# Sample attention of a hybrid decoder layer: the products with the values move one sequence later, in among the next key transposes

## What is computed

```python
def forget_attention(q, k, v, dq, dk, q_pos, k_pos):
    s = jnp.einsum('bqhd,bkhd->bhqk', q, k).astype(jnp.float32) * (HEAD_DIM ** -0.5)
    s = s + jnp.transpose(dq, (0, 2, 1))[..., None] - jnp.transpose(dk, (0, 2, 1))[:, :, None, :]
    mask = k_pos[None, :] <= q_pos[:, None]
    s = jnp.where(mask, s, -jnp.inf)
    p = jax.nn.softmax(s, axis=-1)
    return jnp.einsum('bhqk,bkhd->bqhd', p.astype(v.dtype), v)
...
k_past = cache_k[l][page_table].reshape(Bs, -1, ATT_HEADS, HEAD_DIM)
v_past = cache_v[l][page_table].reshape(Bs, -1, ATT_HEADS, HEAD_DIM)
```

## Time and profile before

| | |
|---|---|
| runs | 2131.2, 2134.02, 2139.19 us (median 2134.02) |
| the profiled execution | 2138.08 us, of which its span is 2136.4 us |
| TensorE busy | 2025.6 us, 95% of the span |
| granted TensorE clock, mean | 0.983 |
| the sample attention | from 409.9 us to 559.0 us of the span |

### The profile page before, as it was taken

One profiled execution on the slowest core, in us unless ns is written; L12 is line 12 of the kernel. 1 busy time (PEld: TensorE's weight loads), 2 busy tenths in 40 slices (PEclk: granted clock), 3 DMA queues, 4 the chain that ended last, 5 costly groups with the idle time before them and its releaser, 6 DMA issues.

```text
span 2136.4 us, 33015 instructions
## 1 busy us (share of the span) xinstructions
PE 2025.6 (95%) x13046; PEld 1926.8 (90%) x13046; DVE 798.0 (37%) x1427; ACT 390.2 (18%) x699; POOL 632.9 (30%) x489
## 2 busy tenths in 40 slices
PE   5989988699999999999999998999999999999996
PEld 4978887555899999999999997999999999999996
DVE  3445556544100224012721667144224423341337
ACT  3434444422100000000210244100000000000003
POOL 4321111023432222223232623432322223232323
PEclk9999998999999999999999999999999999999998
DMA  9322112287422112241111401111111111111112
GB/s 329 102 65 61 39 33 81 93 265 254 149 79 79 50 40 90 70 128 40 39 49 49 155 9 30 50 40 49 39 49 39 49 39 45 43 40 48 40 40 84
DMA packets 174968, 164.17 MB, mean 77 GB/s; under 512 B 14254, under 2 KB 138626, under 8 KB 174747
## 3 DMA queue, kind: packets, MB, share of 16 engines
q1 hardware_dynamic: 153451, 132.50, 20.3%
q0 software_dynamic: 6400, 17.05, 2.5%
q10 hardware_dynamic: 15032, 13.43, 2.0%
HBM read 149.03 MB, written 14.03 MB: 76 GB/s over the span
## 4 chain that ended last, share of the span: by engine, by line
PE 84%; DVE 5%; SPq 4%; ACT 2%; issue 2%; DMA 1%; POOL 0%; ACTq 0%; POOLq 0%; DVEq 0%
PE psA L1767 11%; PE psA L1773 11%; PE psA L1771 11%; PE psB L1773 10%; PE psB L1771 10%; PE psB L1767 10%; PE psB L1881 2%; PE psB L1885 1%; PE psB L1884 1%; PE psA L1935 1%; PE psB L2045 1%; DVE prob L1279 1%; PE ps L1949 1%; PE psA L2020 1%; SPq L405 1%
## 5 line engine op out<-in xcount | busy, mean ns | idle before, releaser
L639 POOL CAST whi<-raw 128x1024 fp32r<-128x1024 f32 x131 | 136.7, 1043 | 1143.2 <-PE psA L1767 547.7
L640 POOL TENSOR_TENSOR wlo<-raw,whi 128x1024 fp32r<-128x1024 f32 x131 | 321.7, 2456 | 10.5
L1767 PE MATMUL psA<-hhi,whi 128*128 128x364 f32 x1008 | 223.3, 330 | 3.0 <-DVE stat L1363 1.6
L1773 PE MATMUL psA<-hhi,wlo 128*128 128x364 f32 x1008 | 223.4, 330 | 0.0
L1771 PE MATMUL psA<-hlo,whi 128*128 128x364 f32 x1008 | 223.1, 329 | 0.0
L1773 PE MATMUL psB<-hhi,wlo 128*128 128x364 f32 x960 | 212.5, 330 | 0.0
L1767 PE MATMUL psB<-hhi,whi 128*128 128x364 f32 x960 | 211.9, 329 | 0.6 <-DVE alo L1388 0.6
L1771 PE MATMUL psB<-hlo,whi 128*128 128x364 f32 x960 | 212.5, 329 | 0.0
L1642 DVE TENSOR_TENSOR ft<-psB,sil 128x1092 f32<-128x1092 f32 x22 | 28.5, 1296 | 405.4 <-PE psB L1773 398.2
L1767 PEld LDWEIGHTS psA<-hhi,whi 128*128 128x128 f32 x1008 | 174.8, 189 | 3.8 <-issue 3.4
L1773 PEld LDWEIGHTS psA<-hhi,wlo 128*128 128x128 f32 x1008 | 175.8, 189 | 0.0
(11 more groups left out here) (419 smaller groups left out, 3639.6 us busy)
## 6 DMA issues: line engine op xcount, KB each, us to landing
raw<-in_w_in SPq DMA_DIRECT2D x53, 512.0 KB, 3.9
raw<-in_w_gate_up SPq DMA_DIRECT2D x44, 512.0 KB, 3.8
kpage<-in_cache_k SPq DMA_DIRECT2D x64, 256.0 KB, 4.4
vpage<-in_cache_v POOLq DMA_DIRECT2D x64, 256.0 KB, 4.0
ada_late<-in_ada_w SPq DMA_DIRECT2D x8, 2048.0 KB, 8.1
raw<-in_w_down SPq DMA_DIRECT2D x22, 512.0 KB, 3.8
ada<-in_ada_w SPq DMA_DIRECT2D x4, 2048.0 KB, 18.0
x_keep<-xt SPq DMA_DIRECT2D x1, 4368.0 KB, 21.6
```

The costliest lines, as they stand in the source:

```text
L639: link(nc.gpsimd.tensor_copy(whi[slot][:, 0:n, :], raw[slot][:, 0:n, :]))
L640: nc.gpsimd.tensor_tensor(wlo[slot][:, 0:n, :], raw[slot][:, 0:n, :], whi[slot][:, 0:n, :].bitcast(F32), ALU.subtract).then_inc(s["w_split ...
L1767: m = mm(ps[:, c, 0:CH], whi[slot][:, b, :], hi[:, k, c * CH:(c + 1) * CH], start=first, stop=False)
L1773: m = mm(ps[:, c, 0:CH], wlo[slot][:, b, :], hi[:, k, c * CH:(c + 1) * CH], start=False, stop=last)
```

## The change

The products with the values run one sequence late. In the loop over b (now 1 to 6) TensorE runs scores(b), key transposes 0 and 1 of b+1, the first half of the values' products **of b-1**, transposes 2 and 3, the second half, transposes 4 and 5, the new rows' product, the probabilities' transposes of b, transposes 6 and 7, and the fold of b-1. Sequence 0 has no values' products before the loop. After the loop stand scores(7), the values' products of 6, the probabilities' transposes of 7, the fold of 6, then the values' products of 7, the `gemm` of `U_BRA` and the fold of 7. In the new-row column block the transposed probabilities go to `psA` bank 2 instead of `psB` bank 1. The copies on ScalarE and VectorE follow the new order. The decay rows of sequences 1 to 7 are issued on ScalarE's queue, after the copies of its sequence, and no more on SyncE's.

```diff
@@ -398,6 +398,13 @@
...
+        def decay_loads(eng, b):
+            for half in range(2):
+                for c, src, w in ((0, half * KH, KH), (KH, PAST, DS)):
+                    eng.dma_start(decs[half * NS:(half + 1) * NS, c:c + w],
+                                  nd_s[bass.ds(b * H, H), None, src:src + w].to_broadcast([H, DS, w])).then_inc(s["dec_in"], 16)
...
@@ -495,25 +502,14 @@
                 apart(sp)
                 page_loads(sp, b, kpage, "cache_k", kpg_in[q], range(2 * q, 2 * q + 2))
-            def decay_loads(b):
-                if not isinstance(b, int) or b:
-                    sp.wait_ge(s["pt_tr"], 2 * b)
-                    apart(sp)
-                for half in range(2):
-                    for c, src, w in ((0, half * KH, KH), (KH, PAST, DS)):
-                        sp.dma_start(decs[half * NS:(half + 1) * NS, c:c + w],
-                                     nd_s[bass.ds(b * H, H), None, src:src + w].to_broadcast([H, DS, w])).then_inc(s["dec_in"], 16)
-            decay_loads(0)
+            decay_loads(sp, 0)
             for q in range(4):
                 key_loads(1, q)
             with sp.Fori(1, DB - 1) as b:
                 key_loads(b + 1, 0)
                 key_loads(b + 1, 1)
-                decay_loads(b)
                 key_loads(b + 1, 2)
                 key_loads(b + 1, 3)
-            decay_loads(DB - 1)
...
@@ -971,7 +967,8 @@
                 act.wait_ge(s["kt_tr"], b * 2 * HP + (g + 1))
                 nc.scalar.copy(kt_group(g), mi[0][:, :].rearrange("p (a b) -> p a b", a=2)).then_inc(s["kt_act"], 1)
-            def sample(b, more):
+            def sample(b, before, more):
                 if more:
                     keys_t(b + 1, 0)
                 act.wait_ge(s["sm_done"], b + 1)
@@ -984,14 +981,24 @@
                 nc.scalar.copy(ptrs[:, 0:NPG // 2, :].rearrange("p a b -> p (a b)"), psB[:, 0, :]).then_inc(s["pt_act"], 1)
                 if more:
                     keys_t(b + 1, 6)
-                act.wait_ge(s["fold_done"], b + 1)
-                nc.scalar.copy(ahi[:, :, bass.ds(b * DS + NP, DS)], att_s).then_inc(s["sah_done"], 1)
+                    act.wait_ge(s["pt_tr"], b * 2 + 2)
+                    apart(act)
+                    decay_loads(act, b + 1)
+                if before:
+                    folded(b)
+            def folded(done):
+                act.wait_ge(s["fold_done"], done)
+                nc.scalar.copy(ahi[:, :, bass.ds(done * DS + (NP - DS), DS)], att_s).then_inc(s["sah_done"], 1)
             for g in range(0, 2 * HP, 2):
                 keys_t(0, g)
-            with act.Fori(0, DB - 1) as b:
-                sample(b, True)
-            sample(DB - 1, False)
+            sample(0, False, True)
+            with act.Fori(1, DB - 1) as b:
+                sample(b, True, True)
+            sample(DB - 1, True, False)
+            folded(DB)
...
@@ -1373,29 +1381,40 @@
                 V.tensor_scalar(decs[:, :], decs[:, :], rowinv[:, 0:1], None, ALU.mult).then_inc(s["sp_done"], 1)
                 if more:
                     keys_t(b + 1, 3)
+                    keys_t(b + 1, 5)
+                if before:
+                    own_heads(b)
                 dve.wait_ge(s["pt_tr"], b * 2 + 2)
-                V.tensor_copy(ptrs[0:DS, NPG // 2, :], psB[0:DS, 1, 0:P]).then_inc(s["pt_dve"], 1)
+                V.tensor_copy(ptrs[0:DS, NPG // 2, :], psA[0:DS, 2, 0:P]).then_inc(s["pt_dve"], 1)
                 if more:
                     queries(b + 1)
-                    keys_t(b + 1, 5)
-                dve.wait_ge(s["ov_done"], b * 2 + 2)
+                    keys_t(b + 1, 7)
+                if before:
+                    folded_low(b)
+            def own_heads(done):
+                dve.wait_ge(s["ov_done"], done * 2)
                 V.tensor_tensor(om[:, :].rearrange("p (h d) -> p h d", h=H), psB[:, 2, :].rearrange("p (h d) -> p h d", h=H),
                                 blockmask[:, :, None].to_broadcast([P, H, HD]), ALU.mult).then_inc(s["om_done"], 1)
-                if more:
-                    keys_t(b + 1, 7)
-                dve.wait_ge(s["sah_done"], b + 1)
-                V.tensor_tensor(alo[:, :, bass.ds(b * DS + NP, DS)], att_s,
-                                ahi[:, :, bass.ds(b * DS + NP, DS)].bitcast(F32), ALU.subtract).then_inc(s["sal_done"], 1)
+            def folded_low(done):
+                at = bass.ds(done * DS + (NP - DS), DS)
+                dve.wait_ge(s["sah_done"], done)
+                V.tensor_tensor(alo[:, :, at], att_s, ahi[:, :, at].bitcast(F32), ALU.subtract).then_inc(s["sal_done"], 1)
             queries(0)
             for g in range(1, 2 * HP, 2):
                 keys_t(0, g)
-            with dve.Fori(0, DB - 1) as b:
-                link.enter(b, 8)
-                sample(b, True)
-            link.leave(DB - 1)
-            sample(DB - 1, False)
+            sample(0, False, True)
+            with dve.Fori(1, DB - 1) as b:
+                link.enter(b - 1, 8)
+                sample(b, True, True)
+            link.leave(DB - 2)
+            sample(DB - 1, True, False)
+            own_heads(DB)
+            folded_low(DB)
...
@@ -2005,11 +2024,10 @@
                         m = tr(mi[g % 2][:, j * P:(j + 1) * P], kpage[:, 2 * (g // 2) + j % 2, at:at + P], ident[:, :])
                     m.then_inc(s["kt_tr"], 1)
-            def sample(b, more):
-                sample_scores(b)
-                sample_values(b, more)
+            hpg = NPG // 2
             def sample_scores(b):
                 pe.wait_ge(s["qbd_done"], b * 3 + 3)
                 pe.wait_ge(s["kt_act"], b * HP + HP)
                 pe.wait_ge(s["kt_dve"], b * HP + HP)
@@ -2021,43 +2039,70 @@
                                    start=k == 0, stop=k == HP - 1)
                 m.then_inc(s["ss_done"], 1)
-            def sample_values(b, more):
-                if more:
-                    keys_t(b + 1, range(5))
-                pe.wait_ge(s["sp_done"], b + 1)
-                apart(pe)
-                for g in range(NPG // 2):
-                    m = tr(psB[:, 0, g * P:(g + 1) * P], decs[:, g * P:(g + 1) * P], ident[:, :])
-                m.then_inc(s["pt_tr"], 1)
-                tr(psB[0:DS, 1, 0:P], decs[:, KH:LR], ident[:, :]).then_inc(s["pt_tr"], 1)
-                if more:
-                    keys_t(b + 1, [5])
-                pe.wait_ge(s["vpg_in"], b * (8 * NPG) + 8 * NPG)
-                pe.wait_ge(s["pt_act"], b + 1)
-                pe.wait_ge(s["pt_dve"], b + 1)
-                hpg = NPG // 2
-                for g in range(hpg):
-                    if g == 2:
-                        m.then_inc(s["ov_done"], 1)
-                        pe.wait_ge(s["vnew_in"], b * (8 * NPG + 16) + 8 * NPG + 16)
+            def sample_values(done, second):
+                if second:
+                    pe.wait_ge(s["vnew_in"], done * (8 * NPG + 16))
+                else:
+                    pe.wait_ge(s["vpg_in"], done * (8 * NPG))
+                    pe.wait_ge(s["pt_act"], done)
+                    pe.wait_ge(s["pt_dve"], done)
+                for g in range(hpg // 2 * second, hpg // 2 * (second + 1)):
                     for half in range(2):
                         rows = slice(half * NS, (half + 1) * NS)
                         m = mm(psB[rows, 2, :], ptrs[:, g, rows], vpage[:, half * hpg + g, :], start=g == 0, stop=half == 0 and g == hpg - 1)
+                if not second:
+                    m.then_inc(s["ov_done"], 1)
+            def sample_new_values():
+                rows = slice(NS, 2 * NS)
                 mm(psB[rows, 2, :], ptrs[0:DS, hpg, rows], vpage[0:DS, NPG, :], start=False, stop=True).then_inc(s["ov_done"], 1)
-                if more:
-                    keys_t(b + 1, [6, 7])
-                pe.wait_ge(s["om_done"], b + 1)
+            def probabilities_t(b):
+                pe.wait_ge(s["sp_done"], b + 1)
+                apart(pe)
+                for g in range(hpg):
+                    m = tr(psB[:, 0, g * P:(g + 1) * P], decs[:, g * P:(g + 1) * P], ident[:, :])
+                m.then_inc(s["pt_tr"], 1)
+                tr(psA[0:DS, 2, 0:P], decs[:, KH:LR], ident[:, :]).then_inc(s["pt_tr"], 1)
+            def sample_fold(done):
+                pe.wait_ge(s["om_done"], done)
                 for k in range(HP):
                     m = mm(att_s[:, k, :], om[:, k * P:(k + 1) * P], fold[:, :], start=True, stop=True)
                 m.then_inc(s["fold_done"], 1)
             keys_t(0, range(2 * HP))
-            with pe.Fori(0, DB - 1) as b:
-                sample(b, True)
+            sample_scores(0)
+            keys_t(1, range(6))
+            probabilities_t(0)
+            keys_t(1, [6, 7])
+            with pe.Fori(1, DB - 1) as b:
+                sample_scores(b)
+                keys_t(b + 1, [0, 1])
+                sample_values(b, 0)
+                keys_t(b + 1, [2, 3])
+                sample_values(b, 1)
```

(15 more changed lines are left out.)

## The result

The changed kernel took 2159.5 us (median of 4 runs, 2156.39 to 2162.35) against 2133.64 us for the kernel before on the same chip (4 runs, 2131.2 to 2139.19). The ratio is 1.0122, with a 95% interval of 1.0106 to 1.0137. Forecast were 2132.7 us and a range to 2140: the change made the kernel slower by 26 us where nothing measurable was expected. The profiled execution has a span of 2158.8 us, 22.4 above the one before.

The account below looks back on a forecast made before the run. The prediction took TensorE's turn, 1.79 us of it waits, as the bound, value loads close second. First sequence -4.8, turns -7.6, end +11.1 gave -1.3 us: 2132.7 us from 2134.02, range 2124 to 2140.

Parts of the forecast that it names:

- the one on the decay rows: On ScalarE's queue rows land 3.8 us after their last issue, about 1.1 us late; TensorE waits 0.3 us a turn.
- R2: Rival: ScalarE's late decay rows bound the turns; at 15.6 us a turn 2138.7 us; chance 0.12 below 0.5%, 0.06 in full.
- The chain behind it: In each turn late decay rows delay VectorE's mask addition and maximum, then group 1's copy, then TensorE's group 3.
- R2's brake: Argument against R2: a turn of 16.6 us, needed for over 0.5% slower, thins the DMA traffic again.
- Traffic, 0.15 us a turn: In the six turns the same bytes go in less time, DMA share 0.82 to 0.89, three queues issuing: 0.15 us each.
- TensorE's own turn: In the six turns, work of 13.92 us plus a 0.2 us tail: 14.15 us a turn.
- The value loads as the second limit: In the turns, value loads of 15.05 us allow a turn of 14.1 us, 15.5 in a slow round.
- R1: Rival: turns reach TensorE's own 14.15 us, 2.7 us more gained, about 2130.0 us; chance 0.25 together with R3.
- R4: Rival: the value loads set the turn at 15 us, total +1 us, 2135 us; chance 0.12.
- The first sequence: Values and fold leave it, the 3.74 us key-page wait stays; scores(1) start 4.8 us earlier (bounds 4 to 5.3).
- The end: From scores(7) to the next `gemm`: 38.8 us against 27.67, value-load waits of 2.7 and 3.6 us; 11.1 us more.
- R3: Rival: last pages land in 2.4 us each and the clock holds; end +8 us, 2129 us; chance 0.25 together with R1.

Follow-up runs that it names:

- the third and fourth experiments: Changed kernel without the value loads of sequences 1 to 7, and changed kernel without the key loads of sequences 2 to 7: 2123.14 us and 2128.24 us.
- the first experiment: Changed kernel with the decay rows back on SyncE's queue, between the key pages of groups 2-3 and 4-5: 2138.21 us, ratio 1.0016.

## Why the prediction was wrong, step by step

**The step that failed** is the one on the decay rows: "How long they need to land: ... so 3.8 us." They took 9.1, 7.2, 7.5, 7.9 and 6.8 us in the turns b = 2 to 6 (in the first turn and the last sequence, with one stream beside them, 4.9 each). The 3.8 us came from a row in which the four issues stood in a pause of both page queues, SyncE's because it was issuing the decay rows itself; the prediction took the number along to a queue and a moment at which both kinds of pages are issued beside them. Its bound above, "1.2 us if they land 0.9 us later", was drawn around that number and not around the state it was measured in. The nearest row for that state stood in the groups: 6.7 us, the longest landing of the earlier trace rows. It was named as R2's condition and given 0.06.

**The chain behind it was right.** The addition, the maximum, group 1's copy, group 3 of TensorE: R2 as written, and that each us of lateness "goes wholly into the turn" holds, as the least that it costs. The mean landing of those five turns is 7.7 us, 3.9 later than taken; 14.6 + 3.9 = 18.5 us a turn. Measured were 20.1. The missing 1.6 us are a second term that the prediction priced only in the first sequence and at the end: in four of those five turns TensorE came back from its wait, of 3.38 to 5.29 us, at 1.2 GHz. There the half of the values behind the wait took 2.96 to 3.68 us and not 1.94; behind the shorter waits of 0.64 and 2.93 us it took 1.94. The group of the key transposes over the six turns gives the wait (busy us, mean ns, idle us ahead and its releaser):

```profile
L2024 PE MATMUL ps<-ident,kpage 128*128 128x128 f32 x192 | 29.6, 296 | 20.0 <-DVE kt_s L1358 20.0
```

20.0 us are the wait, six times for the same copy. TensorE's busy time in the turns is 95.16 us, and 85.78 for the same matmuls in the kernel with the early decay rows, whose clock stayed at 1.00: 9.4 us are the clock. Together they are 29.4 us, and 115.63 less that is 86.2, or 14.4 us a turn.

**R2's brake did not hold.** "Against: a turn that long thins the traffic again": the share over all turns fell to 0.72, but in the stretches from the first decay issue to the addition it was 0.86 to 0.98 in the five turns. An average over a turn said nothing about these 9 to 11 us.

**Traffic, 0.15 us a turn**, was the term that stood for all of this. It was mis-sized by more than twenty times: 3.9 us of landing in each of five turns. It was also put on TensorE's turn and not on the one transfer that has no slack.

**The Trainium skill (DMA: Bandwidth & Descriptors, Anatomy of one DMA — SWDGE (gpsimd) path)** gave an estimate of 2.3 us for the larger decay DMA, by a fit for DMAs that GpSimd issues. The four rows together took 2.4 and 2.5 us where no page was in flight, which is near it (the larger DMA is issued 0.7 us ahead of the last row); they took 4.0 and 4.5 at b = 2 with one stream taken away and 9.1 with both, and there the measurement decides. The Trainium skill (the same page, Issuing engines are not separate DMA queues) says that DMAs of different issuers interleave on the same engines, and the third and fourth experiments agree. By the same section another issuer saves only issue time, and no forecast should stop at that: here, with TensorE's order untouched, the move cost 38 us at one place in ScalarE's queue and nothing at another.

**What was right.** TensorE's own turn, 14.32 where nothing waits (14.15 forecast). The value loads as the second limit at about 15 us: turns of 14.7 to 14.9 in the three kernels with early decay rows, with 0.3 to 1.0 us of waits for the new rows in three to five of the six. So R1 was out of reach and something near R4 would have been the outcome. The first sequence, 14.27 us (15.2), was less near: the wait for key pages that was to stay at 3.74 us came as two, of 1.88 and 1.43, and the groups between them ran at the full clock. The end: 37.56 us (38.8), with these rows, after the earlier trace rows:

```profile
552.64 1.94 PE L2053 MATMUL psB<-vpage,ptrs 128*64 128x512 f32 x8 [1.58 <-DMA vpage<-out_v_sample]
...
561.57 6.66 PE L2053 MATMUL psB<-vpage,ptrs 128*64 128x512 f32 x16 [4.15 <-DMA vpage<-in_cache_v]
...
569.15 0.77 PE L1786 MATMUL psA<-hhi,whi 128*128 128x364 f32 x3
```

The wait of 1.6 us for sequence 6 is as forecast. For sequence 7 two waits of 2.7 and 3.6 us were forecast; there was one of 4.15, after which all 16 products ran at the lower clock (6.66 us), slowly enough that the second half's rows came in time. The sum is the same within 1.2 us, by another split, and so in part by luck. R3 did not come about.

**The forecast's sum**, made with the pieces of the kernel with early decay rows, is -5.8 - 6.3 + 12.7 = +0.6 us, and that kernel's median of 2130.49 us is 3.5 below the one before: the forecast's range would have held for a change whose decay rows had no part in it.

**Open** stays why the landing is 9.1 us in one turn and 6.8 in another, and by what mechanism two streams of pages slow a third DMA so much more than one does, since the share of the DMA engines alone doesn't sort the landings. Open is also how much of the first experiment's faster landings (4.1 to 6.7) comes from the key pages that SyncE doesn't issue beside them and how much from two issuers instead of three.

## What to carry to other kernels

A landing time belongs to what was in flight when it was measured: before a DMA is moved to another queue or moment, look at which queues were silent at its old place, and price it by the longest landing of the trace under the traffic of the new one. Look for a queue's pauses in narrow windows, for one merged row can hide them. If a tile can be freed early enough to ask for its data most of a turn ahead, the queue stops mattering. And the four longest of TensorE's waits in the turns were paid twice here, once as the wait and once as the slower products behind it.

## What the runs showed of the hardware

- Two DMAs of 128 KB with their narrow pair, from ScalarE's queue and counted from the last issue, took 2.4 and 2.5 us to land with no pages in flight, 4.0 to 5.3 with one stream of 256 KB pages beside them, and 5.1 to 9.1 with both streams (6.8 to 9.1 in the changed kernel). From SyncE's queue, between its own key pages and with value pages beside them, they took 4.1 to 6.7.
- After waits of 3.38 to 5.29 us TensorE ran the value products that followed at 1.2 GHz (2.96 to 3.68 us for eight, not 1.94); after one of 2.93 it did not. In two other kernels it did after waits of 3.06, 2.76 and 2.46 us (2.90 to 3.47 us for eight), and didn't after one of 2.45, so the length of the wait alone doesn't tell.
